# Opening the layer by halves of the features, constants on SyncE's queue, and u copied out by ScalarE

## The reference, cut to what matters

```
mod = silu(cond) @ w_ada + b_ada                         # 6 x 1024 for each of the two request groups
h = rmsnorm(x, g_pre_mix) * (1.0 + scale_a) + shift_a
z = h @ w_in                                             # u, q, k, v, o (512 columns each) and 16 gate columns
y_pool = pool_mixer(u, w_pool, pool_scale, grid)         # four windows, four groups of 128 columns
y_ml, C, n, m = mlstm_mixer(q, k, v, o, gate_pre, ...)   # forward and backward scan, 4 heads
x = x + gate_a * rmsnorm(concat(y_pool, y_ml) @ w_out, g_post_mix)
h = rmsnorm(x, g_pre_ffn) * (1.0 + scale_f) + shift_f
f = moe(h, ...)                                          # 64 experts, 6 of them per token, and a shared one
x = x + gate_f * rmsnorm(f, g_post_ffn)
```

## Time and profile before

| | |
|---|---|
| median of 3 runs | 757.88 us (756.28 to 759.22) |
| profiled execution: its own time | 755.75 us |
| its span | 753.7 us |
| busy in the span | PE 702.0, DVE 404.3, ACT 190.4, POOL 84.6 us |
| chain that ended last | PE 72%, DVE 12%, DMA 10%, ACT 3% |
| L1144, sums of the modulation on VectorE | 72 operations into PSUM, 48.2 us, mean 750 ns |
| L1207, u out of PSUM by VectorE | 1.88 us for three |
| L837, a PSUM bank of 128x512 out by ScalarE | 0.58 us |
| DMA issue of w_ada on SyncE, 2048 KB, median to landing | 16.2 us |

### The profile page before, as it was taken

How to read it: one execution, slowest core, us unless ns; L and a number is a source line. 1 busy time by engine, 2 the same in 40 slices (tenths; PEclk the granted TensorE clock), 3 DMA queues, 4 the chain that set the end, 5 groups by cost and what they waited for, 6 DMA issues and landing times.

```text
span 753.7 us, 11427 instructions
## 1 busy us (share of the span) xinstructions
PE 702.0 (93%) x4241; PEld 405.5 (54%) x4241; DVE 404.3 (54%) x1004; ACT 190.4 (25%) x320; POOL 84.6 (11%) x49
## 2 busy tenths in 40 slices
PE   1779999999989999999999999999999999997995
PEld 1579888688866645544444444444444444442332
DVE  3078999577084754554544545455444546333444
ACT  3144413474264112211111111112111111110113
POOL 2244444411400100000000000000000000000000
PEclk9979999999999999999999999999999999999998
DMA  9998476533669659869999999999999999999992
GB/s 325 379 383 271 170 261 240 195 143 97 211 227 424 271 199 411 327 264 428 427 423 422 429 423 421 427 424 424 424 427 424 428 420 430 424 424 419 421 372 95
DMA packets 49708, 259.14 MB, mean 344 GB/s; under 512 B 6513, under 2 KB 9169, under 8 KB 30705
## 3 DMA queue, kind: packets, MB, share of 16 engines
q1 hardware_dynamic: 41664, 249.05, 81.7%
q0 software_dynamic: 1808, 5.92, 2.2%
q10 hardware_dynamic: 6176, 3.40, 1.6%
HBM read 254.64 MB, written 3.71 MB: 343 GB/s over the span
## 4 chain that ended last, share of the span: by engine, by line
PE 72%; DVE 12%; DMA 10%; ACT 3%; SPq 1%; issue 1%; ACTq 0%; DVEq 0%
PE psum L2069 23%; PE psum L2081 11%; PE psum L1963 9%; DMA w_gu<-in_w_expert_gu 8%; PE psum L2041 8%; PE psum L529 4%; PE psum L531 4%; PE psum L530 4%; DVE psum L1144 3%; DMA w_gu<-in_w_ada 3%; PE psum L1944 3%; DVE f_acc L1551 2%; PE psum L1975 1%; SPq L647 1%; PE psum L2028 1%
## 5 line engine op out<-in xcount | busy, mean ns | idle before, releaser
L2069 PE MATMUL psum<-w_gu,hgT 128*32 128x512 f32 (+1 forms) x1280 | 192.7, 600 | 5.0 <-DMA w_gu<-in_w_expert_gu 5.0
L1551 DVE TENSOR_TENSOR f_acc<-f_acc,psum 128x512 f32<-128x512 f32 x156 | 106.1, 687 | 44.9 <-PE psum L2041 41.4
L2069 PEld LDWEIGHTS psum<-w_gu,hgT 128*32 128x32 f32 (+1 forms) x1280 | 58.5, 120 | 131.1 <-issue 131.0
L2081 PE MATMUL psum<-w_dn,actT 128*32 128x512 f32 (+1 forms) x640 | 98.5, 596 | 0.5 <-ACT actT L965 0.5
L1536 DVE SCALAR_TENSOR_TENSOR act<-sil,wsl,psum 128x256 f32<-128x256 f32 x27 | 18.4, 680 | 130.8 <-ACT sil L990 124.8
L2041 PE MATMUL psum<-y_hi,onehotT 128*128 128x512 f32 x156 | 67.8, 435 | 4.6 <-DVE f_acc L1551 2.5
L524 POOL TENSOR_TENSOR w_lo<-w_gu,w_hi 128x2048 fp32r<-128x2048 f32 x14 | 64.3, 4600 | 64.7 <-ACT w_hi L754 64.7
L1963 PE MATMUL psum<-onehot,h_hi 128*128 128x512 f32 (+1 forms) x168 | 67.3, 401 | 0.0
L1963 PE MATMUL psum<-onehot,h_lo 128*128 128x512 f32 (+1 forms) x168 | 64.9, 386 | 0.0
L1542 DVE TENSOR_TENSOR y_lo<-psum,y_hi 128x1024 fp32r<-128x1024 f32 x27 | 33.0, 1224 | 54.1 <-ACT y_hi L994 54.1
L2041 PE MATMUL psum<-y_lo,onehotT 128*128 128x512 f32 x156 | 61.2, 392 | 0.0
(11 more groups left out here) (293 smaller groups left out, 865.7 us busy)
## 6 DMA issues: line engine op xcount, KB each, us to landing
w_gu<-in_w_expert_gu SPq DMA_DIRECT2D x49, 2048.0 KB, 19.4
w_dn<-in_w_expert_down SPq DMA_DIRECT2D x64, 1024.0 KB, 17.8
w_gu<-in_w_expert_gu SPq DMA_DIRECT2D x30, 1024.0 KB, 14.5
w_gu<-in_w_ada SPq DMA_DIRECT2D x12, 2048.0 KB, 16.2
w_gu<-in_w_in SPq DMA_DIRECT2D x4, 2048.0 KB, 9.0
w_gu<-in_w_out SPq DMA_DIRECT2D x2, 2048.0 KB, 9.1
bc<-mod_rows POOLq DMA_DIRECT2D x6, 512.0 KB, 7.4
w_gu<-in_w_in SPq DMA_DIRECT2D x2, 1024.0 KB, 15.1
```

The costliest lines, as they stand in the source:

```text
L1551: v.tensor_tensor(dst, dst, bank(5 + n), ALU.add).then_inc(f_added, 1)
L2069: ins = t.matmul(bank(2)[rows, :], column(c)[:, rows], w_gu[s][:, c, :], start=(c == 0), stop=(c == NC - 1), tile_position=(0, rows.start))
L2081: ins = t.matmul(bank(3 + n)[rows, :], actT[:, j, rows], w_dn[s][:, j, 512 * n:512 * (n + 1)], start=(j == 0), stop=(j == 1), tile_positio ...
```

## The change

- SyncE's loads and the buffers: a2 before a1, and the chunk q between a2 and a1, so that q takes the third buffer; q is loaded as two halves with a1 and a3 between. a5 takes the buffer of q and is issued behind v. The seven loads of constants are issued by SyncE behind a6.
- The first half of the features (groups 0 to 3) needs only a0 and a2, the second a1 and a3: `modulation(half)` on VectorE and `modulation_T(half)` on TensorE stand for the old single step. TensorE does a1 behind the first half's transposes of the rows, a3 ahead of q's third unit, and the second half's transposes of rows ahead of q's fourth.
- Shifts: VectorE does groups 0 to 2 and 4 to 6, ScalarE 3 and 7. PARTS has four pairs.
- GpSimd makes the low part of q's first half ahead of its five small DMAs.
- The third unit of q goes to bank 0, the gates to bank 6. VectorE has the whole of a5's sums behind the gates' chain.
- ScalarE copies u out of PSUM, behind the rounding of w0's first half, once four totals are summed.

```diff
         COL = {"u": 0, "q": MW, "k": 2 * MW, "v": 3 * MW, "o": 4 * MW}
-        order = ["a0", "a1", "a2", "a3", "q", "a4", "a5", "k", "v", "a6", "a7", "o", "u", "a8", "a9",
+        order = ["a0", "a2", "q", "a1", "a3", "a4", "a5", "k", "v", "a6", "a7", "o", "u", "a8", "a9",
                  "w0", "w1", "a10", "a11", "s"]
...
                    + [("o", i) for i in range(NT)] + [("u", i) for i in range(NT)])
-        by_act = [n for n, (w, _) in enumerate(z_units) if w in "qko"]
-        by_dve = [n for n, (w, _) in enumerate(z_units) if w in "vu"]
+        by_act = [n for n, (w, _) in enumerate(z_units) if w in "qkou"]
+        by_dve = [n for n, (w, _) in enumerate(z_units) if w == "v"]
...
             w, i = z_units[n]
-            return (1, 2, 6, 7)[i] if w == "q" else 2 + i
+            return (1, 2, 0, 7)[i] if w == "q" else 2 + i
...
-        PARTS = ((0, 2), (2, 4), (4, 8))
+        PARTS = ((0, 2), (2, 4), (4, 6), (6, 8))
+        ON_ACT = (3, 7)
...
                 sp.dma_start(x[:, i, :], src).then_inc(x_in, 16)
-            a7, o = chunk["a7"], chunk["o"]
-            for name in order[:a7] + ["o", "a7"] + order[o + 1:]:
+            def constants_of_mixer():
+                sp.dma_start(poolm[:, :, :].rearrange("p g n -> p (g n)"), t_in["pool_constants"]).then_inc(pool_in, 16)
+                sp.dma_start(w_pool[:, :, :], t_in["w_pool"][0].rearrange("g c e -> c g e")).then_inc(pool_in, 16)
+                sp.dma_start(c0n[:, :, 0:DH], t_in["state_C"][0, 0].rearrange("d h k v -> k (d h) v")).then_inc(state_in, 16)
+                with nc.allow_non_contiguous_dma(reason="a few hundred single values"):
+                    sp.dma_start(pool_scale, t_in["pool_scale"][0].rearrange("(g e) -> e g", e=P)).then_inc(pool_in, 16)
+                    sp.dma_start(c0n[:, :, DH:DV].rearrange("p r o -> p (r o)"),
+                                t_in["state_n"][0, 0].rearrange("d h k -> k (d h)")).then_inc(state_in, 16)
+                sp.dma_start(w_router[:, :, :], t_in["w_router"][0].rearrange("(p c) n -> p c n", c=NC)).then_inc(router_in, 16)
+                sp.dma_start(b_router[:, :], t_in["b_router"][0:1, :].broadcast_to([P, NE])).then_inc(router_in, 16)
+
+            issued = ["a0", "a2", "q", "a1", "a3", "q", "a4", "k", "v", "a5", "a6", "o", "a7"] + order[chunk["u"]:]
+            for turn, name in enumerate(issued):
                 i = chunk[name]
...
                     sp.wait_ge(gu_used[s], i // PSLOTS)
+                if name == "q" and "q" in issued[turn + 1:]:
+                    sp.dma_start(w_gu[s][:, 0:NC // 2, :], chunk_source(name)[:, 0:NC // 2, :]).then_inc(q_in, 16)
+                    continue
                 if name == "q":
-                    sp.dma_start(w_gu[s][:, 0:NC // 2, :], chunk_source(name)[:, 0:NC // 2, :]).then_inc(q_in, 16)
                     sp.dma_start(w_gu[s][:, NC // 2:NC, :], chunk_source(name)[:, NC // 2:NC, :]).then_inc(gu_in[s], 16)
...
                 sp.dma_start(w_gu[s][:, :, :], chunk_source(name)).then_inc(gu_in[s], 16)
+                if name == "a6":
+                    constants_of_mixer()
                 if name == "s":
...
             def high_tokens(first, end):
-                if first < 4:
-                    a.wait_ge(h1_dve, 2 * end)
-                else:
-                    a.wait_ge(h1_act, NC)
+                here = [c for c in range(end) if c in ON_ACT]
+                a.wait_ge(h1_dve, 2 * (end - len(here)))
+                if here:
+                    a.wait_ge(h1_act, 2 * len(here))
                 a.activation(tT_hi[first // 4][:, first % 4:end - 4 * (first // 4), :], hT[:, first:end, :], ACT.Copy)\
...
             a.wait_ge(modT_ready, 1)
-            shifted(4)
-            shifted(5)
+            shifted(3)
             high_tokens(*PARTS[0])
-            shifted(6)
             high_tokens(*PARTS[1])
             high(1)
+            a.wait_ge(modT_ready, 2)
             shifted(7)
             high_tokens(*PARTS[2])
-
...
+            high_tokens(*PARTS[3])
...
                     a.activation(kT[:, i, :], bank(z_bank(n), 0, T), ACT.Copy, scale=DH ** -0.5).then_inc(z_act, 1)
+                elif w == "u":
+                    a.activation(u_tok[:, i, :], bank(z_bank(n)), ACT.Copy).then_inc(z_act, 1)
                 else:
...
                             g_b[32 * d:32 * d + H, T_CTX - 1:T_CTX]).then_inc(m_out, 16)
-            a.wait_ge(mod_a_ready, 1)
+            a.wait_ge(mod_a_ready, 2)
             for m in range(2):
...
             high(10)
+            a.wait_ge(ada_summed, 4)
+            for n in range(14, 17):
+                z_evac(n)
             high(11)
...
-            for i in (0, 2, 1, 3):
-                ada_evac(i)
-            v.wait_ge(mod_ready, 4)
-            one_plus(2, 0).then_inc(mod_a_ready, 1)
-            v.wait_ge(modT_done, 1)
-            v.tensor_copy(modT[:, :, :, :].rearrange("p a c m -> p (a c m)"), bank(6, P, P + 32)).then_inc(modT_ready, 1)
-            v.wait_ge(modT_ready, 1)
+            def modulation(half):
+
+                ada_evac(half)
+                ada_evac(2 + half)
+                v.wait_ge(mod_ready, 2 * half + 2)
+                v.scalar_tensor_tensor(modrow[:, 2 + half, :], modrow[:, 2 + half, :], 1.0, grow[:, 0, half, :],
+                                       ALU.add, ALU.mult).then_inc(mod_a_ready, 1)
+                v.wait_ge(modT_done, half + 1)
+                v.tensor_copy(modT[:, :, 4 * half:4 * half + 4, :],
+                              bank(6, P, P + 32).rearrange("p (a c m) -> p a c m", a=2, c=NC)[:, :, 4 * half:4 * half + 4, :])\
+                    .then_inc(modT_ready, 1)
+                v.wait_ge(modT_ready, half + 1)
...
             def shifted(c):
+                if c + 1 in ON_ACT:
+                    v.wait_ge(h1_act, 2 * ON_ACT.index(c + 1) + 2)
                 for m, (lo, hi) in enumerate(((0, T_CTX), (T_CTX, T))):
...
-            shifted(0)
-            shifted(1)
-            shifted(2)
-            low_tokens(0)
-            shifted(3)
-            low_tokens(1)
-            low_tokens(2)
+            for half in range(2):
+                modulation(half)
+                for c in range(4 * half, 4 * half + 3):
+                    shifted(c)
+                low_tokens(2 * half)
+                low_tokens(2 * half + 1)
...
                     if i == 4:
-                        v.wait_ge(h1_act, NC)
+                        v.wait_ge(h1_act, 2 * len(ON_ACT))
                     elif i == 5:
...
             ada_sums(4)
-            ada_sums(5, 0, 3)
...
             for b, dst in enumerate((g_in, g_lf)):
-                own.add(v.tensor_scalar(dst[0:32, :], bank(0, 0, T)[64 * b:64 * b + 32, :], b_gate[0:32, b:b + 1], None, ALU.add))
+                own.add(v.tensor_scalar(dst[0:32, :], bank(6, 0, T)[64 * b:64 * b + 32, :], b_gate[0:32, b:b + 1], None, ALU.add))
                 for tile in range(NT):
                     ins = v.tensor_scalar(dst[32:36, P * tile:P * tile + P],
-                                          bank(0, 0, T)[64 * b + 32:64 * b + 36, natural(1, tile)],
+                                          bank(6, 0, T)[64 * b + 32:64 * b + 36, natural(1, tile)],
                                           b_gate[32:36, b:b + 1], None, ALU.add)
...
             v.tensor_tensor(g_b[:, :], g_b[:, :], g_mx[:, :], ALU.add).then_inc(scans_ready, 1)
-            ada_sums(5, 3)
+            ada_sums(5)
             v.wait_ge(scans_ready, 1)
...
             ada_sums(9)
-            for n in range(14, 17):
-                wait_unit(v, n)
-                v.tensor_copy(u_tok[:, z_units[n][1], :], bank(z_bank(n))).then_inc(z_dve, 1)
             for i in range(8, 10):
...
+            low(g, 0)
             g.wait_ge(gu_in[3], 16)
...
-            for k in range(12):
+            for k in range(1, 12):
                 low(g, k)
...
             ada(0)
-            ada(1)
             t.wait_ge(const_in, 16)
...
             ada(2)
-            ada(3)
-            t.wait_ge(mod_a_ready, 1)
-            for i in range(4):
-                ins = t.matmul(bank(6, P + 8 * i, P + 8 * i + 8), modrow[:, i, :],
-                               ident.rearrange("p (j r) -> p j r", j=4)[:, :, 0:2], start=True, stop=True)
-            ins.then_inc(modT_done, 1)
+
+            def modulation_T(half):
+                t.wait_ge(mod_a_ready, half + 1)
+                if half:
+                    t.wait_ge(modT_ready, half)
+                for i in (half, 2 + half):
+                    ins = t.matmul(bank(6, P + 8 * i, P + 8 * i + 8), modrow[:, i, :],
+                                   ident.rearrange("p (j r) -> p j r", j=4)[:, :, 0:2], start=True, stop=True)
+                ins.then_inc(modT_done, 1)
+
+            modulation_T(0)
+            ada(1)
...
                     if w == "q":
-                        t.wait_ge(tl_ready, 1 if half == 0 else len(PARTS))
```

(14 more changed lines are left out.)

9 lines of the change are left out of this document (removed).

## The result

The changed kernel took 748.33 us (median; 745.07 to 749.72) against 757.21 us for the kernel before on the same chip (756.28 to 759.22): ratio 0.9878, 95% interval 0.9855 to 0.9902. The profiled execution took 748.34 us (span 746.2), against 755.75 (753.7) before, so the two traces differ by 7.4 us. In a second session it took 749.52 against 756.28, ratio 0.9921 (0.9891 to 0.9951), which is 6.8 us and just inside the range.

What follows compares the result with a forecast made beforehand. TensorE and VectorE, tied in the opening, bound the kernel; k's earlier start moves everything behind it. 4.5 us from that plus 0.1 from u make 4.6: 755.75 to 751.2, plus 2.1 to the runs' median: 753.3, range 749.0 to 757.8.

Steps and rivals of the forecast that it cites:

- G: Start of k's matmuls on TensorE, 66.47 us before; forecast at 62.0, 4.5 us earlier, moving everything behind it.
- I take it as held: First half's scaling STT on VectorE: due at 26.1 behind GpSimd's start at 25.6, held, done at 30.4.
- The second hold: Second half's scaling STT on VectorE: due at 43.0, held 0.9 us by GpSimd's subtraction from 39.3 to 43.9.
- rival (a): Opening: neither scaling STT held, clock up throughout; k starts at 57.9, gain 8.6, time 749.3; chance 0.15.
- Rival (c): TensorE's pause between q's halves lowers its clock, up to 2.9 us; gain 2.1, time 755.8; chance 0.20.
- Part 2: a5 loaded late: negation reached at G + 9.8, before GpSimd; no wait at v's end; cost 0, or 1.7.
- rival b: VectorE's negation L1179 still meets GpSimd; TensorE waits 1.7 us at v's end; time 755.0; chance 0.15.
- Part 3: Seven constants' loads issued by SyncE instead of ScalarE, some 13 us: worth 0 by itself, but lets G move.
- Part 4: Three copies of u moved from VectorE to ScalarE: between 0 and 0.6 us, taken as 0.1.
- the two ends, 139.42 and 139.31, are a tenth apart: Opening's ends on TensorE and VectorE before the change, read as tied: relieving one alone brings nothing.
- The base: Profiled execution 755.75, less 4.6, gives 751.2; raised 2.1 to the runs' median 757.88, giving 753.3.
- the distance from G to the span's end: Sign of error: everything behind k's start should take 687.2 us, within a microsecond.

Runs made afterwards that it cites:

- the repeat: The changed kernel itself, unaltered, timed again in a second session beside the kernel before: 749.52 us against 756.28, ratio 0.9921.

## Why the prediction was wrong

The mechanism, an earlier k that carries everything behind it, was right. G's gain of 6.32 us was still there at w_out's issue (6.31) and nearly whole at w_shared_gu's (6.60: 0.76 more by u's part, 0.47 less by a lapse of the clock). The sizes were not.

**The step that failed: "I take it as held".** Against the profiled execution the forecast was 751.2 and the measurement 748.34, 2.9 us off, and 1.85 of them are G (62.0 against 60.15). GpSimd's first start was right within 0.3 us (25.36 for 25.6), and the price of a hold nearly (4.24, 4.12 and 4.50 us for "up to 4.0"). What was wrong was the order: the STT ran at 24.30, not 26.1. The transposes and a2's matmuls all came at their short times (2.84 and 1.95), so a2 ended at 23.6; I had taken 25.5 out of 24.1 to 28.7, and even the low end was too high. The hold was then not 4.3 us long but absent, and q started at 32.6 instead of 35.1.

The second hold was gone as well. a3's matmuls ended at 38.9 for 42.4: 2.5 of these 3.5 us are q's earlier start, 1.0 is TensorE's clock, which was up from q's first matmuls on (0.17 to 0.20 apart from 32.85, where I had it change at 37.6). That alone would not have done: the forecast had GpSimd's second start at 39.3 and wrote that the hold stands "unless a3's matmuls end before 38.7". The STT came at 39.50, and it won because q's second half landed 1.1 us late and GpSimd started at 40.39. So the second race was won by luck, as the repeat, which lost it by 0.19 us, shows. This is rival (a), to which I gave 0.15.

By the rule of the Trainium skill, page "SBUF — State Buffer", section "Who interferes with whom", the two exclude each other if they overlap; the experiments agree, with 4.24 us against 0.29. The rule does not say which of the two comes first in this kernel, and there the forecast went by one side of a gap of 0.5 us. It should have carried both orders at both places: at the second the same kernel runs in both, 0.89 us ahead in one execution and 0.19 us behind in another.

**Rival (c) came too.** The pause was 2.15 us (2.0 forecast) and the clock fell: 11 matmuls at 0.32, 1.6 us (up to 2.9 forecast). Rival (a) had q's end at 53.3. The second half started 1.0 us later than (a) had it (45.93 for 44.9): its first low part, ready to go at 44.35, was held to GpSimd's end (1.43 us for 0.95), and that end was 44.96 for 43.9, the same late landing. (c)'s 1.6 came on top, and the gates take 4.2: 60.1, the measured G. I had kept the two as separate cases, and their sum was what happened. a4's sums, which forecast and (a) had as the last to arrive, ended at 58.6 and held nothing up.

**Part 2** held in every row: the negation at G + 9.65 (forecast G + 9.8) took 0.35 us, 0.9 ahead of GpSimd; the copy took 2.68 (2.4); TensorE did not wait for modrow at v's end. Its border was real as well: with the gates in the pause the negation started 0.7 us behind GpSimd and took 4.59, and TensorE waited 2.09 us at v's end (1.7 in rival b).

**Part 3**: "worth 0 by itself, but it is what lets G move" is what the two runs show (ratio 1.0009 alone, and 1.0018 for all else without it). Only the issue was longer, 17 us for 13, with 8.62 for one load of single values; o's load at 76.99 was still in time.

**Part 4, the second mis-sized term.** I took 0.1 us; the traces give 0.76, and 2.3 in executions without the lapse. The step that failed is the first reading of all: "the two ends, 139.42 and 139.31, are a tenth apart". They were so because TensorE's clock had been low from 103 to 107 us in that one execution. Without the lapse TensorE is ready 1.5 us sooner and VectorE's tail decides. The granted clock of that stretch stands in the trace before; the forecast didn't use it.

**The base.** 2.1 us of the forecast came from lifting the profiled sum to the median of the three runs, 757.88. In later sessions the kernel before had medians of 756.22 (31 runs), 756.28 (20), 756.27 (17) and 756.24 (11), so 1.6 of the 2.1 was the scatter of three runs. The changed kernel's own medians, 748.33 and 749.52, lie on either side of the range's lower end; the step above had failed whichever of them one takes, as G and the two STTs show.

I had also said that I would be wrong if the distance from G to the span's end was not 687.2 within a microsecond. It was 686.05: 0.76 less by part 4, 0.47 more behind it by the lapse at 145 us, and 0.9 less, by the spans, from w_shared_gu's load on. The last is open beyond what is said above: it parts the profiles in two groups, and not by kernel alone. Why q's second half landed 1.1 us late is open too. So is whether the lapse behind the narrow matmuls follows from them: it stands there in 6 of 16 profiles, each time starting 2.3 to 3.4 us behind the first of them, but no run took them away. That the slower of the two groups of runs in some variants are lost races is shown for two profiled runs (757.90, with the first of its holds forced, and 760.25; three holds each) and argued for the others.
